# A hybrid decoder layer on one core: stick-breaking attention weights by a running product on VectorE, with the value products ahead of filler and transposes

## The reference

```python
# q, k, v: (B,S,8 heads,64); in blocks of 128 queries
z = jnp.einsum('bthd,bshd->bhts', qi, kf) * scale          # scale = 1/8
causal = kpos[None, :] < tpos[:, None]                     # strictly earlier keys
log_keep = jnp.where(causal, jax.nn.log_sigmoid(-z), 0.0)
later = lax.cumsum(log_keep, axis=3, reverse=True) - log_keep
w = jnp.where(causal, jnp.exp(jax.nn.log_sigmoid(z) + later), 0.0)
y = jnp.einsum('bhts,bshd->bthd', w, vf)
```

## Time and profile before

| | |
|---|---|
| median of three runs | 2296.27 us |
| profiled execution | 2296.45 us, span 2294.5 us |
| mean granted clock of TensorE in it | 0.961 |
| busy: TensorE, VectorE, ScalarE, GpSimd | 91%, 41%, 36%, 4% |
| attention stage on TensorE | 168.4 to 608.0 us |

### The profile page before, as it was taken

How to read it: one execution, slowest core, us unless ns; L and a number is a source line. 1 busy time by engine, 2 the same in 40 slices (tenths; PEclk the granted TensorE clock), 3 DMA queues, 4 the chain that set the end, 5 groups by cost and what they waited for, 6 DMA issues and landing times.

```text
span 2294.5 us, 26913 instructions
## 1 busy us (share of the span) xinstructions
PE 2094.6 (91%) x9758; PEld 1633.1 (71%) x9758; DVE 940.9 (41%) x1291; ACT 824.3 (36%) x1322; POOL 101.7 (4%) x71
## 2 busy tenths in 40 slices
PE   7998888888899999999979899978999999999994
PEld 5875555555577787878748688836888888888883
DVE  5614544545452624445214555245323322323335
ACT  5325655656542434334313333333202212212211
POOL 0000000000011020302000000020000000000002
PEclk9998999999999999999989999978999999999997
DMA  4221121111220302121042544211111111111113
GB/s 157 102 73 60 48 80 69 41 69 41 78 101 19 119 30 107 37 73 55 30 181 92 201 143 147 89 80 46 46 54 47 46 46 47 53 46 46 53 39 146
DMA packets 52762, 174.16 MB, mean 76 GB/s; under 512 B 5744, under 2 KB 5744, under 8 KB 52720
## 3 DMA queue, kind: packets, MB, share of 16 engines
q1 hardware_dynamic: 51568, 171.52, 21.0%
q10 hardware_dynamic: 1152, 2.10, 0.2%
HBM read 127.45 MB, written 46.14 MB: 76 GB/s over the span
## 4 chain that ended last, share of the span: by engine, by line
PE 75%; DVE 8%; ACT 5%; issue 4%; DMA 4%; POOL 1%; SPq 1%; ACTq 0%; DVEq 0%; POOLq 0%
PE gemm L324 18%; PE gemm L326 18%; PE gemm L325 18%; PE dn L1198 2%; PE dn L1196 2%; PE gemm L1277 2%; DMA w_raw<-w_stream 2%; PE gemm L1278 1%; PE gemm L1279 1%; PE attn_out L1128 1%; ACT w_hi L311 1%; DVE d_cv L1465 1%; PE z L1099 1%; DMA a_k<-projections 1%; DVE a_sp_lo L1422 1%
## 5 line engine op out<-in xcount | busy, mean ns | idle before, releaser
L324 PE MATMUL gemm<-act_hi,w_hi 128*128 128x512 f32 x1472 | 612.6, 416 | 23.7 <-DVE act_lo L505 10.2
L326 PE MATMUL gemm<-act_hi,w_lo 128*128 128x512 f32 x1472 | 583.8, 397 | 0.0
L325 PE MATMUL gemm<-act_lo,w_hi 128*128 128x512 f32 x1472 | 583.2, 396 | 0.0
L324 PEld LDWEIGHTS gemm<-act_hi,w_hi 128*128 128x128 f32 x1472 | 282.3, 192 | 97.1 <-issue 29.7
L316 DVE TENSOR_TENSOR w_lo<-w_raw,w_hi 128x1024 fp32r<-128x1024 f32 x142 | 175.1, 1233 | 366.7 <-ACT w_hi L311 361.7
L326 PEld LDWEIGHTS gemm<-act_hi,w_lo 128*128 128x128 f32 x1472 | 281.5, 191 | 61.8
L325 PEld LDWEIGHTS gemm<-act_lo,w_hi 128*128 128x128 f32 x1472 | 282.9, 192 | 56.8 <-issue 6.5
L311 ACT ACTIVATE w_hi<-w_raw 128x1024 fp32r<-128x1024 f32 x142 | 149.3, 1051 | 328.6 <-PE gemm L326 281.5
L324 PE MATMUL gemm<-f_hi,w_hi 128*128 128x512 f32 x512 | 199.2, 389 | 0.0
L325 PE MATMUL gemm<-f_lo,w_hi 128*128 128x512 f32 x512 | 199.2, 389 | 0.0
L326 PE MATMUL gemm<-f_hi,w_lo 128*128 128x512 f32 x512 | 199.2, 389 | 0.0
(11 more groups left out here) (252 smaller groups left out, 2762.7 us busy)
## 6 DMA issues: line engine op xcount, KB each, us to landing
w_raw<-w_stream SPq DMA_DIRECT2D x142, 512.0 KB, 3.6
projections<-stage SPq DMA_DIRECT2D x60, 512.0 KB, 2.9
gate<-projections SPq DMA_DIRECT2D x48, 256.0 KB, 2.7
d_in<-projections SPq DMA_DIRECT2D x12, 512.0 KB, 4.5
y_lo<-branch_outputs SPq DMA_DIRECT2D x6, 1024.0 KB, 12.0
x_sb<-xT SPq DMA_DIRECT2D x8, 512.0 KB, 9.3
x_fin<-xT SPq DMA_DIRECT2D x4, 1024.0 KB, 8.6
residual<-mixed SPq DMA_DIRECT2D x8, 512.0 KB, 2.7
```

What stands on the lines that cost most here:

```text
L324: nc.tensor.matmul(g_bank[hf][:], w_hi[s][:, k, :], a_hi[:, k, t], start=(k == 0), stop=False)
L325: nc.tensor.matmul(g_bank[hf][:], w_hi[s][:, k, :], a_lo[:, k, t], start=False, stop=False)
L326: last = nc.tensor.matmul(g_bank[hf][:], w_lo[s][:, k, :], a_hi[:, k, t], start=False, stop=(k == KT - 1))
```

## The change

Scores are laid out the other way: 128 queries on the partitions, up to 512 keys in the free dimension. ScalarE makes b = sigmoid(z/8) and keep = 1 - b. VectorE forms the product of all later keeps by one scan from the last key to the first (`tensor_tensor_scan`, multiply, then maximum with a floor that is 1 beyond the diagonal and 0 elsewhere), multiplies it with b, and masks the diagonal 128 columns. TensorE transposes the weights 128 columns at a time, ScalarE copies them out of PSUM, and TensorE multiplies them with the values in chunks of 128 keys. In a round of TensorE's loop come: scores two blocks ahead, the value products of the block before, filler, the transposes of this block, filler. Query blocks go in the order 4, 5, 6, 7, 3, 2, 1, 0; the 12 blocks of a round have 128, 512, 256, 512, 384, 512, 512, 512, 512, 384, 256 and 128 columns. SyncE loads the next round's inputs within the round, and the first round's in the phase before; it passes the first phase end without waiting for the last stores, and waits for them behind it. The result y is copied by VectorE, 128 columns at a time. Removed functions are not shown in full:

```diff
+    a_b = [sb(f"a_b{s}", [P, HALF]) for s in range(4)]
+    a_keep = [sb(f"a_keep{s}", [P, HALF]) for s in range(4)]
+    a_P = [[sb(f"a_P{u}{s}", [P, S + 1]) for s in range(2)] for u in range(2)]
+    a_A = [sb(f"a_A{s}", [P, HALF]) for s in range(4)]
+    a_AT = [[sb(f"a_AT{u}{s}", [P, HALF]) for s in range(2)] for u in range(2)]
+    a_floor = sb("a_floor", [P, S])
+    a_past = sb("a_past", [P, P])
+    a_y = sb("a_y", [P, S])
...
-cum_bank = [c_bank, d_bank[0]]
-s_bank = [z_bank[0], z_bank[1], d_bank[1]]
+y_bank = [o_bank, c_bank]
...
+ORDER = (4, 5, 6, 7, 3, 2, 1, 0)
+BLOCKS = [(p, s0) for p, b in enumerate(ORDER) for s0 in ((HALF, 0) if b >= 4 else (0,))]
 NBK = len(BLOCKS)
-STEPS = [(T, u, j) for T, j in BLOCKS for u in range(2)]
-NST = len(STEPS)
-
-def first_col(T, j):
-    return max(0, P * j - HALF * T)
-
-def cols_of(y):
-    return slice(first_col(STEPS[y][0], STEPS[y][2]), HALF)
-
-def opens(T, j):
-    return j == 4 * T + 3
-
-def is_diag(T, j):
-    return j >= 4 * T
-
-RESTS = [sum(STEPS[v][2] > 0 for v in range(y)) for y in range(NST + 1)]
-N_REST = RESTS[NST]
-LAG = 4
+NST = 2 * NBK
+LEAD = 2
+def block_of(x):
+    p, s0 = BLOCKS[x]
+    b = ORDER[p]
+    end = P * b + P
+    n = min(HALF, end - s0)
+    return b, p, s0, n, S - end + s0
...
+AT_SLOTS = [2.0, 2.0, 3.0, 3.0]
+for x in range(NBK):
+    near = [block_of(v)[3] / HALF for v in range(x, x + LEAD + 1) if v < NBK]
+    AT_SLOTS += [0.4 + 2.0 * sum(near) / len(near)] * 2
+AT_SLOTS += [1.0, 1.0]
...
+        if n == N_PRE:
+            sp.wait_ge(stored[0], 1 + 16 * (n + 1))
+            sp.dma_start(a_q[:], pT[ROW_SQ]).then_inc(at_loaded, 16)
+            sp.dma_start(a_k[:], pT[ROW_SK]).then_inc(at_loaded, 16)
+            sp.dma_start(a_vT[:], pT[ROW_SV]).then_inc(vT_loaded, 16)
+    end_phase(sp, 1)
...
+    with sp.Fori(0, 3) as i:
+        sp_block(sp, PAIR_AT + 2 * i, 0)
+        sp.wait_ge(at_vt, 2 * i + 2)
+        sp.dma_start(a_vT[:], pT[i + 1 + ROW_SV]).then_inc(vT_loaded, 16)
+        sp_block(sp, PAIR_AT + 2 * i, 1)
+        sp_block(sp, PAIR_AT + 2 * i + 1, 0)
+        sp.wait_ge(z_ready, NST * i + NST)
+        sp.dma_start(a_q[:], pT[i + 1 + ROW_SQ]).then_inc(at_loaded, 16)
+        sp.dma_start(a_k[:], pT[i + 1 + ROW_SK]).then_inc(at_loaded, 16)
+        sp_block(sp, PAIR_AT + 2 * i + 1, 1)
+    for b in range(4):
+        sp_block(sp, PAIR_AT + 6 + b // 2, b % 2)
...
+        def sigmoid(y):
+            n = block_of(y // 2)[3]
+            act.wait_ge(z_ready, NST * i + y + 1)
             if y >= 4:
-                act.wait_ge(arg_ready, NST * i + y - 3)
-            nc.scalar.activation(a_z[y % 4][:, cols_of(y)], s_bank[y % 3][:, cols_of(y)], ACT.Copy, scale=0.125).then_inc(z_read, 1)
-
-        def exp_z(y):
-            e = a_e[y % 3][:, cols_of(y)]
-            act.wait_ge(na_ready, NST * i + y + 1)
-            nc.scalar.activation(e, e, ACT.Exp).then_inc(e_ready, 1)
-
-        def ln_z(y):
-            e = a_e[y % 3][:, cols_of(y)]
-            act.wait_ge(e_ready, NST * i + y + 1)
-            nc.scalar.activation(e, e, ACT.Ln, bias=1.0).then_inc(l_ready, 1)
-
-        def upper_sp(y):
-            act.wait_ge(sp_ready, NST * i + y + 1)
+                act.wait_ge(a_ready, NST * i + y - 3)
+            nc.scalar.activation(a_b[y % 4][:, 0:n], z_bank[y % 2][:, 0:n], ACT.Sigmoid, scale=0.125).then_inc(b_ready, 1)
...
+        def keep(y):
...
+            nc.scalar.activation(a_keep[y % 4][:, 0:n], a_b[y % 4][:, 0:n], ACT.Identity, scale=-1.0, bias=1.0).then_inc(keep_ready, 1)
...
+        def take_turned(y):
+            x, u = divmod(y, 2)
+            n = block_of(x)[3]
+            act.wait_ge(turned, NST * i + y + 1)
+            act.wait_ge(av_done, 1 + NBK * i + x - 1)
+            nc.scalar.activation(a_AT[u][x % 2][:, 0:n], d_bank[u][:, 0:n], ACT.Copy).then_inc(at_read, 1)
...
+        for x in range(-LEAD, NBK + 1):
+            if x + LEAD < NBK:
+                for u in range(2):
+                    sigmoid(2 * (x + LEAD) + u)
+            if x == -LEAD:
+                for hf in range(2):
+                    act.wait_ge(at_vt, 2 * i + hf + 1)
+                    act.wait_ge(av_done, 1 + NBK * i)
+                    nc.scalar.activation(a_v[:, 4 * hf:4 * hf + 4, :], d_bank[hf][:].rearrange("p (n c) -> p n c", c=P),
+                                         ACT.Copy).then_inc(at_v, 1)
+            for u in range(2):
+                if x + LEAD < NBK:
+                    keep(2 * (x + LEAD) + u)
+                if 0 <= x < NBK:
+                    take_turned(2 * x + u)
             act_beside(act, b)
+            act_beside(act, b)
+            if x == LAST_OF[3] + 3:
+                store_y(1)
+        store_y(0)
...
+                nc.tensor.matmul(z_bank[u][:, 0:n], a_q[h, P * blk:P * blk + P], a_k[h, s0:s0 + n],
+                                 start=True, stop=True).then_inc(z_ready, 1)
...
+        def turn(y):
+            x, u = divmod(y, 2)
+            n = block_of(x)[3]
+            pe.wait_ge(a_ready, NST * i + y + 1)
+            if x == 0:
+                pe.wait_ge(at_v, 2 * i + u + 1)
+            else:
+                pe.wait_ge(at_read, 1 + NST * i + y - 1)
+            for m in range(n // P):
+                last = nc.tensor.transpose(d_bank[u][:, P * m:P * m + P], a_A[y % 4][:, P * m:P * m + P], ident)
+            last.then_inc(turned, 1)
...
         def weighted_values(x):
...
+            pe.wait_ge(at_read, 1 + NST * i + 2 * x + 2)
+            if newest(x):
+                pe.wait_ge(av_read, 2 + 8 * i + p - 1)
+            for m in range(n // P):
+                for u in range(2):
+                    last = nc.tensor.matmul(y_bank[p % 2][64 * u:64 * u + 64, 0:P], a_v[:, s0 // P + m, 64 * u:64 * u + 64],
+                                            a_AT[u][x % 2][:, P * m:P * m + P], start=(newest(x) and m == 0),
+                                            stop=(oldest(x) and m == n // P - 1), skip_group_check=True)
...
+        for x in range(-LEAD, NBK + 1):
+            if x + LEAD < NBK:
+                scores(x + LEAD)
+            if x == -LEAD:
+                turn_values()
+            if x >= 1:
+                weighted_values(x - 1)
             pe_beside(pe, b)
+            if 0 <= x < NBK:
+                turn(2 * x)
+                turn(2 * x + 1)
+            pe_beside(pe, b)
...
+        def product_of_later(y):
+            x, u = divmod(y, 2)
+            blk, p, s0, n, off = block_of(x)
+            run = a_P[u][p % 2]
+            dve.wait_ge(keep_ready, NST * i + y + 1)
+            if not newest(x):
+                dve.wait_ge(p_ready, NST * i + y - 1)
+            floor = a_floor[:, S - n:S] if newest(x) else a_floor[:, 0:n]
+            nc.vector.tensor_tensor_scan(run[:, off:off + n][:, ::-1], a_keep[y % 4][:, 0:n][:, ::-1], floor[:, ::-1],
+                                         run[:, off + n:off + n + 1], ALU.mult, ALU.max).then_inc(p_ready, 1)
...
+        def weigh(y):
+            x, u = divmod(y, 2)
+            blk, p, s0, n, off = block_of(x)
+            dve.wait_ge(p_ready, NST * i + y + 1)
+            if y >= 4:
+                dve.wait_ge(turned, NST * i + y - 3)
+            nc.vector.tensor_tensor(a_A[y % 4][:, 0:n], a_b[y % 4][:, 0:n], a_P[u][p % 2][:, off + 1:off + n + 1],
+                                    ALU.mult).then_inc(a_raw if newest(x) else a_ready, 1)
+        def mask(y):
+            x, u = divmod(y, 2)
+            n = block_of(x)[3]
+            dve.wait_ge(a_raw, RAWS[NBK] * i + RAWS[x] + u + 1)
+            a = a_A[y % 4][:, n - P:n]
+            nc.vector.tensor_tensor(a, a, a_past[:], ALU.mult).then_inc(a_ready, 1)
+        def take_y(p):
+            blk = ORDER[p]
+            dve.wait_ge(av_done, 1 + NBK * i + LAST_OF[p] + 1)
+            dve.wait_ge(y_stored[blk // 4], 1 + 16 * i)
+            nc.vector.tensor_copy(a_y[:, P * blk:P * blk + P], y_bank[p % 2][:, 0:P]).then_inc(av_read, 1)
+        for x in range(-LEAD, NBK + 1):
+            for p in range(8):
+                if LAST_OF[p] == x - 2:
+                    take_y(p)
+            if 0 <= x + 1 < NBK:
+                for u in range(2):
+                    product_of_later(2 * x + 2 + u)
+                for u in range(2):
+                    weigh(2 * x + 2 + u)
+                if newest(x + 1):
+                    for u in range(2):
+                        mask(2 * x + 2 + u)
             dve_beside(dve, b)
+            dve_beside(dve, b)
+        take_y(7)
...
```

More of the change, by code:

```diff
@@ L602, in _ @@
                     sp_block(sp, i, s, early=True)
-            with sp.Fori(N_PRE, N_SB) as i:
+            for n in range(N_PRE, N_SB):
                 for s in range(2):
-                    sp_block(sp, i, s)
+                    sp_block(sp, n, s)
+                if n == N_PRE:
[4 more added lines that the diff above has]
+            end_phase(sp, 1)
             for s in range(2):
                 sp.wait_ge(stored[s], 1 + 16 * N_SB)
```

(26 more changed lines are left out.)

160 lines of the change are left out of this document (27 added, 133 removed).

## The result

2170.6 us (median of four, 2167.5 to 2173.2) against 2295.95 before: a ratio of 0.9453, interval 0.9436 to 0.9469, 125 us less. The forecast was 2165 in a range of 2152 to 2208. The profiled execution took 2169.72 us, span 2167.8, against 2296.45.

What follows compares the result with a forecast made beforehand. TensorE, busy 91% of the span, was taken as the bound. Four attention rounds of 76.5 us plus 2.0 make 308.0 against 439.6, so -131.6 from 2296.45 gives 2165 us, range 2152 to 2208.

Steps and rivals of the forecast that it cites:

- Removed work: Attention round: 88 running-sum products (15.3 us), 16 masking products (1.1), waits for a_sp_lo, and load waits between rounds go.
- the new sum: TensorE's attention round: filler 43.5, scores 10.8, value products 10.9, weight transposes 7.9, value transposes 0.9: 74.0 us; 76.5 with extras.
- its 0.8 for the clock: Attention round: 0.8 us added because the dense delta-rule stage is granted a clock of 0.99.
- the rival of the hand-overs: Attention blocks: TensorE waits about 1 us more at each of 12 value products; 88.5 us a round, 2213; chance 0.15.
- The seam: Stretch between attention rounds, 10.2 us before: next loads issued a round earlier and covered; one 128-column score group, eight transposes stay.
- the term for ScalarE's first sigmoid: Start of the next attention round: ScalarE waits for the last y copy, first sigmoids end at 4.4 against 4.1; 0.3 to 0.4 us.
- The scan: VectorE in attention: 512 scan between 0.68 and 1.29 us, upper end taken; VectorE 49 us a round, hidden.
- Both cases with VectorE as the bound: Attention round set by slow scans: still faster, 93 us, 2231, chance 0.04; or slower, 2325 at 10 ns per element, chance 0.04.
- The margin behind the transposes: 512 block: ScalarE free of its copies at 2.5 us, TensorE at value products at 3.7; margin 1.2 us.
- The clock: Attention stage: 0.98 or more expected; rival, it falls as often as now (0.93), 82.3 us a round, 2188, chance 0.11.
- The two ends: Attention stage: 1.2 us wait for the first sigmoid at the start, release of SP's queue 0.8 us later at the end.
- the signs on record: Attention: period 76 to 77 us, no load waits, clock 0.98, 512 scans 1.2 to 1.3, VectorE and ScalarE 45 to 50.

Runs made afterwards that it cites:

- the groups side by side: Changed kernel with scores, value products and transposes of a block next to each other, both filler slots behind them (block 0 keeps one ahead): 2171.9 us.
- the order the other way: Changed kernel with TensorE's order turned to scores, transposes of this block, filler, value products of the block before, filler: 2176.2 us.
- the filler ahead: Changed kernel with both filler slots of a block ahead of the transposes and none behind: 2193.7 us.

## Why the prediction was right

- What bounds the kernel: right. TensorE is busy for 305 of 311 us. Doubling its transposes costs in full, doubling VectorE's scans nothing.
- Removed work and the new sum: right. The rows carried over: eight transposes 0.79 us, a 512 score group 1.06. Four chunks took 1.02 where the count had 1.15: entering them from scores costs nothing. A round without a fall of the clock, less the wait of 1.76 at the seam, is 75.8 us; the sum had 76.1 without its 0.4 at the seam. That they agree so well is in part luck: its 0.8 for the clock was not needed in such a round, which is granted 1.00, and all that comes on top of the 74.0 took 1.8 where it had 1.3. That nothing in the stage waits for ScalarE's copies settles the rival of the hand-overs.
- The seam: the loads are covered, as forecast, but the term for ScalarE's first sigmoid (0.3 to 0.4 us) was mis-sized: 1.76. It counted a table load for the first round only and took it that the set stays from round to round. The kernel before names its set ahead of the loop and shows one load there; the new one names none and loads at each round's head. The run with the load ahead of the loop gives back 1.3 us a round, 3.4 us in the time, of the 5.6 by which 2165 was short.
- The scan: taken at the upper of two ends, 1.29 us for 512, measured 1.27; its four widths lie on 2.1 ns per element, and `weigh` on 1.0. The Trainium skill, "DVE: opcode table, instruction layouts, handler registers and perf-mode slots", section "6. Datapath and trigger behaviour", has the built-in scan at half throughput; the trace agrees, with 2.1 against 1.0 ns. Both cases with VectorE as the bound fell with it: they needed 2.9 and 4.7 us.
- The margin behind the transposes: right in place. Taken away, it costs waits of 5.4 us a round, 4.6 of them for the copies, for the 8 of the same count.
- The clock: granted 0.99 in the stage, 1.00 with twice the transposes. What lowers it here is a wait: in the changed kernel's stage the one stretch at half rate stands behind a wait of 1.75 us at a seam. The sentence of the Trainium skill, "TensorE: Matmul & The Clock Gate", section "Part 4: PE-mode transpose", that these don't count as TensorE being busy, was weighed as a rival; what it would do to the clock is not seen here, since transposes never stand alone for long.
- The two ends: 1.2 us of waiting at the start was 0.4; SyncE's queue was released 5.7 us after TensorE's last product, not later than before (6.0 by the same count). Together 1.9 us too dear, which hid a part of the miss at the seams.
- The total: in the profiled run the stage is 2.9 us longer than the 308.0 of the sum, and the rest of the program, forecast to shift only, took 2.0 more. Of the signs on record one failed: VectorE and ScalarE are busy for 43.7 and 41.4 us of a round (245.7 to 323.3), not for 45 to 50.

## What to carry to other kernels

When one engine is full and the others are half empty, price the new work on the full one by the distance from start to start of the nearest form, and count every change between groups. Where others only have to keep up, write down how long the slowest hand-over takes and which work stands in its way, and look at the loop's head for what an engine does anew in each round, table loads first.

## What the runs showed of the hardware

- Whether an activation table is loaded in each round depended on what stands ahead of the loop: one named load there, and four of 1.28 us within the loop were gone.
- From filler to value products (64 columns) costs TensorE about 0.1 us, as does the way back; from scores (64 rows) or value products to transposes it is 0.06 us, and from scores to value products nothing. Why is not shown.
- A wait of 1.75 us in an otherwise full TensorE was followed by 1.2 GHz for about 3.4 us, at 1.6 us of cost: at one of three seams in one profile, at none in a second profile of the same kernel, and at all three with the groups side by side. Of the other runs with this wait the doubled scans and the order the other way show it at one seam, the tripled scans at two, the doubled transposes and the filler ahead at none. A wait of 0.5 us at a seam was never followed by it.
- Two profiles of the same kernel had the attention stage begin 4.5 us apart (165.0 and 169.5), while undisturbed rounds agree to 0.01 us.
